# VectorE in the place of GpSimd for the low parts of the feed-forward chunks

## The reference, cut to what matters

```python
def swiglu(h, w_gu, w_down):
    g, u = jnp.split(h @ w_gu, 2, axis=-1)
    return (jax.nn.silu(g) * u) @ w_down

x = x + 0.5 * rmsnorm(swiglu(rmsnorm(x, g_pre), w_gu, w_down), g_post)   # twice
```

## Time and profile before

| | us |
|---|---|
| median of 3 runs | 1805.03 |
| lowest, highest | 1803.73, 1808.21 |
| the profiled execution | 1803.31 |
| its span (first to last instruction) | 1801.5 |

### The profile page before, as it was taken

The page is one execution under the profiler, slowest core; times in us unless marked ns, Lnnn a source line. Parts: engine busy times, 40 slices in busy tenths (PEclk is TensorE's granted clock), DMA queues, the critical chain, the costliest instruction groups (busy, mean ns, idle before and its releaser), DMA issues.

```text
span 1801.5 us, 33894 instructions
## 1 busy us (share of the span) xinstructions
PE 1763.6 (98%) x12118; PEld 1606.1 (89%) x12118; DVE 1159.3 (64%) x2216; ACT 847.5 (47%) x1294; POOL 827.8 (46%) x337
## 2 busy tenths in 40 slices
PE   9999999999999999999998999999999999999998
PEld 8899987888989998968998999999998888888997
DVE  6866766575353347647575999999995555544444
ACT  5444532556464445595344554544443333344444
POOL 4666685733756664700006789300014444444442
PEclk9999999999999999999999999999999999999999
DMA  7555443522445553532554555433345555555553
GB/s 272 216 181 186 175 153 125 192 95 87 173 150 186 186 187 107 198 117 96 175 186 156 173 186 175 159 129 126 127 140 188 187 190 192 188 186 177 187 186 114
DMA packets 84929, 297.64 MB, mean 165 GB/s; under 512 B 10244, under 2 KB 13733, under 8 KB 84582
## 3 DMA queue, kind: packets, MB, share of 16 engines
q1 hardware_dynamic: 82688, 290.82, 47.8%
q10 hardware_dynamic: 2150, 5.57, 0.9%
HBM read 295.30 MB, written 1.05 MB: 165 GB/s over the span
## 4 chain that ended last, share of the span: by engine, by line
PE 64%; issue 15%; POOL 12%; DVE 6%; ACT 1%; DMA 1%; POOLq 0%; SPq 0%; DVEq 0%; ACTq 0%
POOL ring_lo L541 12%; PE ps L1848 10%; PE ps L1850 10%; PE ps L1849 10%; PE ps L2353 7%; PE ps L2354 6%; PE ps L2355 6%; PE ps L2389 2%; PE ps L2076 2%; PE ps L1963 2%; PE ps L1964 2%; PE ps L1965 2%; DVE ring_lo L1185 1%; PE ps L2044 1%; DMA ring<-in_stream 1%
## 5 line engine op out<-in xcount | busy, mean ns | idle before, releaser
L1850 PE MATMUL ps<-h_hi,ring_lo 128*128 128x256 f32 (+1 forms) x2432 | 684.6, 281 | 0.0
L541 POOL TENSOR_TENSOR ring_lo<-ring,peer_split 128x1024 fp32r<-128x1024 f32 x128 | 315.7, 2466 | 464.1 <-ACT peer_split L655 458.4
L1850 PEld LDWEIGHTS ps<-h_hi,ring_lo 128*128 128x128 f32 x2432 | 458.8, 189 | 0.0
L541 POOL TENSOR_TENSOR ring_lo<-ring,main_hi 128x1024 fp32r<-128x1024 f32 x113 | 283.6, 2510 | 189.3 <-ACT main_hi L655 181.7
L655 ACT ACTIVATE peer_split<-ring 128x1024 fp32r<-128x1024 f32 x256 | 270.2, 1056 | 206.0 <-PE ps L2355 205.9
L541 POOL TENSOR_TENSOR ring_lo<-ring,more_hi 128x1024 fp32r<-128x1024 f32 x87 | 227.5, 2615 | 298.6 <-ACT more_hi L655 292.4
L1848 PE MATMUL ps<-h_hi,peer_split 128*128 128x256 f32 x1024 | 292.0, 285 | 3.4 <-POOL ring_lo L541 2.1
L1849 PE MATMUL ps<-h_lo,peer_split 128*128 128x256 f32 x1024 | 287.5, 281 | 0.0
L655 ACT ACTIVATE main_hi<-ring 128x1024 fp32r<-128x1024 f32 x159 | 167.7, 1058 | 128.6 <-DMA ring<-in_stream 101.5
L1848 PE MATMUL ps<-h_hi,main_hi 128*128 128x256 f32 (+1 forms) x776 | 221.9, 286 | 1.1 <-DVE arena L1328 0.7
L1849 PE MATMUL ps<-h_lo,main_hi 128*128 128x256 f32 (+1 forms) x776 | 218.2, 281 | 0.0
(11 more groups left out here) (414 smaller groups left out, 3349.8 us busy)
## 6 DMA issues: line engine op xcount, KB each, us to landing
ring<-in_stream SPq DMA_DIRECT2D x550, 512.0 KB, 3.3
arena<-in_decay ACTq DMA_DIRECT2D x1, 1536.0 KB, 9.2
x<-in_x SPq DMA_DIRECT2D x4, 256.0 KB, 5.3
arena<-in_keys ACTq DMA_DIRECT2D x1, 1024.0 KB, 5.5
out<-h SPq DMA_DIRECT2D x4, 256.0 KB, 2.6
aux<-in_dft ACTq DMA_DIRECT2D x1, 816.0 KB, 4.5
aux<-in_idft ACTq DMA_DIRECT2D x1, 768.0 KB, 6.0
arena<-in_mask ACTq DMA_DIRECT2D x1, 768.0 KB, 6.6
```

What stands on the lines that cost most here:

```text
L541: nc.gpsimd.tensor_tensor(ring_lo[:, c % NS, :], ring[:, c % NS, :], hi_part(c).bitcast(F32), ALU.subtract).then_inc(lo_pool, 1)
L1850: return M(out, w_lo, parts[0], start=False, stop=stop, skip_group_check=True)
```

## The change

In both feed-forward blocks VectorE makes the low part of every chunk from the fifth on (r >= 4). GpSimd's loop over these chunks is gone; it goes from chunk 3 on to the chunks of the next stage. VectorE makes chunk 5 after the second activation, and in turn m chunks 3m, 3m + 1 and 3m + 2, all ahead of the turn's activation (and of the angle work, where there is some). TensorE's counts in the loops follow: VectorE makes six low parts in a loop pass of two turns, in the place of two.

```diff
@@ _split_plan
-            elif name in ("ffn1", "ffn2") and r >= 4 and r % 3 == 1 or name == "ffn1" and r < 2:
+            elif name in ("ffn1", "ffn2") and r >= 4 or name == "ffn1" and r < 2:
                 who = "dve"
@@ GpSimd
             def ffn(base, first):
                 for r in range(first, 4):
                     lo(base + r)
-                with pool.Fori(0, (FT - 2) // 2) as i:
-                    for m in (2, 3):
-                        lo(base + 3 * m - 1, i, 6, 4)
-                        lo(base + 3 * m, i, 6, 4)
-                lo(base + 3 * FT - 1)
@@ VectorE
                 def turn_of(m, i=0, step=0):
-                    lo(base + 3 * m + 1, i, 3 * step, step)
+                    for r in range(3 * m, 3 * m + 3):
+                        lo(base + r, i, 3 * step)
...
                 one(f * FT + 1, base + 2, 0)
                 one(f * FT + 2, base + 4, 1)
+                lo(base + 5)
...
                     for m in range(2, 12):
-                        lo(base + 3 * m + 1)
+                        for r in range(3 * m, 3 * m + 3):
+                            lo(base + r)
@@ TensorE
                 def turn(m, i=0, step=0):
...
-                    first(m, m % 2, i, 2 * step)
+                    first(m, m % 2, i, 3 * step)
...
-                    second(m - 1, (m - 1) % 2, False, False, i, step)
+                    second(m - 1, (m - 1) % 2, False, False, i, 3 * step)
```

## The result

The changed kernel takes 1811.92 us (median of 6 runs, 1810.98 to 1812.52), the kernel before 1805.68 us in the same comparison (6 runs, 1803.73 to 1808.21): ratio 1.0033, 95% interval 1.0023 to 1.0042. It is slower by 6.2 us, at the bound of what the prediction called no change. The forecast was 1808.5, the range 1804.0 to 1812.5: the sign was right and the time lies inside the range, but the loss is almost twice the +3.5 us of the sum.

A forecast was written before the change was run, and what follows sets the result against it. TensorE, busy 98% of the span, was taken as the bound. Terms -0.9 + 1.05 + 0.7 + 2.7 gave +3.55 us, so 1805.0 + 3.5 = 1808.5 us; range 1804.0 to 1812.5.

The forecast's parts named there:

- Steady state at nothing: Feed-forward turns: VectorE's added low parts, 1.22 us alone, fit within each 8.44 us turn, so no cost.
- Term 1: First block, near 75.6 us: TensorE's one wait for VectorE's low part goes, -0.9 us.
- Term 2: First block, chunk 5 near 26 us: its low part, made behind the second activation, comes late, +1.05 us.
- Term 3: First block, chunk 12 near 46 us: low part stands behind an activation delayed by a DMA landing, +0.7 us.
- Term 4: Second block, chunk 5 near 523 us: low part stands behind an activation waiting for silu, +2.7 us.
- Rival (a): Behind chunk 5 of the second block: a wait above about 1.9 us halves TensorE's clock, 1810.2 to 1812.0; chance 0.25.
- the prediction's own signs of being wrong: Changed trace: TensorE waits in steady turns, a half-clock stretch behind 525 us, or a wait at 523 us under 1 us.
- Cost at nothing: Last chunks and later stages: added low parts fill idle time, GpSimd's earlier freedom gains nothing, DMAs stay; 0 us.
- The lock: Two-input SBUF VectorE instructions and GpSimd's alternate at one port pair; subtractions without GpSimd beside them take 1.22, not 3.21 us.

The follow-up runs named there:

- e3: The changed kernel with VectorE making chunk 5's low part ahead of the second activation in both blocks; 1807.81 us, ratio 1.0015.
- e7: The changed kernel with e3's edit, and GpSimd's third gate-chunk low part only after the first attention head is mixed; 1806.16 us, ratio 1.0000.
- e9: e7 with GpSimd's fourth gate-chunk low part made only after the second attention head is mixed; 1806.48 us, ratio 1.0007.
- e8: The kernel before, with only GpSimd's third gate-chunk low part waiting until the first attention head is mixed; 1811.54 us, ratio 1.0034.
- e2: The change in the second feed-forward block alone, the first as in the kernel before; 1808.35 us, ratio 1.0018.
- e4: The changed kernel with GpSimd's third gate-chunk low part waiting for VectorE's two small scalings in the attention stage; 1812.59 us, ratio 1.0040.
- e5: The changed kernel with 38 already satisfied waits in GpSimd's program where its block 1 loop had stood; 1811.75 us, ratio 1.0031.
- e6: The changed kernel with GpSimd's third gate-chunk low part made only after the first attention head is mixed; 1809.79 us, ratio 1.0027.
- e1: The change in the first feed-forward block alone, the second as in the kernel before; 1808.67 us, ratio 1.0022.

## Why the prediction was right in sign and short in size

- **Steady state at nothing: right**, on its own reason: low parts of 1.22 us (median 1.218 in both blocks), 607 and 604 matmuls in 85 us.
- **Term 1, -0.9: right**, measured -0.96.
- **Term 2, +1.05: right**, measured +1.15. The 1.14 us a low part, for which the prediction names, is not to be read there, but the changed trace has it.
- **Term 3, +0.7: mis-sized**, measured 0. The landing moved by 0.6 of 1.15 us, and the term sat behind term 2; with term 2 taken away it measures 0.5 us in e3 and 1.1 and 1.4 in e7 and e9, inside its bounds of 0 to 1.8. That place moves by itself: e8, which has the order of before there, lost 1.6 us at it.
- **Term 4, +2.7: 0.3 to 0.7 us too large**, measured 2.0 here and 2.0 to 2.4 in e2, e4, e5 and e6; here silu moved less than TensorE did. It was inside its bounds of 0.6 to 3.7.
- **Rival (a)** came true in the profiled execution: +1.5 us at 529.5, in the foreseen place with nearly the foreseen price, and with it one of the prediction's own signs of being wrong. Its condition, a wait above 1.9 us, was wrong: 1.75 us had it, and 2.07 us in e2 did not. Of five traces with this order one has it, so in the median it is a part of its price; e3 against the changed kernel gives 4.1 us for terms 2 and 4 and this stretch together, where their rows give 1.15 + 2.03 + 1.5 = 4.7, less the 0.5 of term 3 that appears.
- **The step that failed is "Cost at nothing"**, which says of GpSimd's earlier freedom "no gain, and none comes later" and sets no loss against it. I took the rest of the kernel as rigid. It is not: GpSimd's low parts and VectorE's small instructions stand in a relation that 0.3 us decides. The shift of TensorE did not decide it: e3 stands 0.1 us ahead of the kernel before at 350 us and has the collision, e2 stands 0.7 us behind it and has not. GpSimd's shorter pause did, 0.16 us for 0.50. The row to see the danger by was in the trace of before: a 128x4 scaling of 1.14 us beside its sister of 0.17. The lock itself stood in the prediction, as a reason why the added subtractions run fast; I did not ask where else GpSimd meets VectorE. Cost: 3.25 us in the profile, 1.7 for the wait and 1.5 for the clock behind it. The repairs gave back 1.7 to 2.1 us in medians (e7 under e3, e6 under the changed kernel). By their traces that is the clock, since one collision is left in either and still costs 1.6 to 1.8 us; no run has the change without any.
- **The range held in part by luck.** It reached up to 1812.5 for rival (a) alone. What filled it is mostly the attention stage, which has no term. And of the 3.4 us between the forecast and the measured time 0.7 are the base: the median of the kernel before was 1805.0 us then and 1805.7 in the comparison.

With these corrections the sum by the profile is 0.2 + 1.15 - 0.96 + 3.25 + 0.4 + 2.03 + 1.5 + 0.6 = 8.2 us. The median's 6.2 are shown in two parts by the repairs: e3 gives back 4.1, e7 1.7 more, and e7 stands at the kernel before within 0.1%. How many of the 6.2 us are half clock stays open, since only one execution of each kernel has a trace. Open is why GpSimd's pause ahead of its third low part shrank from 0.50 to 0.16 us; e1, e2, e5 and e8 only show that it goes with GpSimd's loop in block 1, not with the moment and, if my count is right, not with the bytes of GpSimd's program.

## What to carry to other kernels

When work is taken from an engine, look behind it too for places where a short VectorE instruction on SBUF stands beside GpSimd's long ones, since a fraction of a microsecond between the two decides there. Instructions of one form with durations of 0.17 and 1.1 us in one trace are the sign. The price is up to one GpSimd instruction a collision on whatever waits for it, and two can follow one another (e4, e8). A wait that moves GpSimd's instruction out of the way can move the collision to the next gap too short for it, as in e4, e7 and e9, so check the whole series first. And when work goes to an engine that runs in order, try it ahead of the instruction that waits, not behind: that one line (e3) was worth 4.1 us of the 6.2.

## What was not expected of the hardware

- VectorE's RECIPROCAL on 128x4 numbers took 0.17 us at 361.46 in e8, wholly inside a GpSimd subtraction (361.38 to 363.79), and the TENSOR_SCALAR on 128x2 right behind it took 2.15. At a like size the form of the instruction decides whether GpSimd stops it: over the eleven traces 35 RECIPROCALs ran inside a GpSimd subtraction, none for more than 0.25 us.
- A TENSOR_SCALAR on small numbers that starts within 0.005 us of GpSimd's instruction (351.97 and 351.96 before, 352.62 and 352.62 in e2, 361.38 and 361.38 in e8) takes 0.17 us; 0.33 us behind it, 2.08. Over the eleven traces 107 of them, with 2 to 16 numbers a partition, started 0.026 us or more behind GpSimd's and at least 0.1 us ahead of its end, and all 107 ended 0.02 to 0.05 us behind that end. Those on one number a partition (0.14 to 0.15 us) were not stopped.
- Of TensorE's waits of 1.75 to 2.12 us at these two places, two (1.75 us in the changed kernel, 1.83 in e2) had a half-clock stretch of 3.4 us behind them, and five had none: 1.84 before, 2.07 in e2, 1.77 in e4, 2.00 in e5 and 2.12 in e6, the last four at chunk 5 of block 2.
